# A new order of work in the first block of a transformer-layer kernel

## The reference

```
mod = silu(c) @ ada_w + ada_b                # 6 x 1024: shift1, scale1, gate1, shift2, scale2, gate2
h   = rms_norm(x, norm1_g) * (1 + scale1) + shift1
p   = h @ w_in                               # 1024 x 5384
q, k, v, f_logit, p_rwkv, gate_logit = split(p)   # 512, 512, 512, 8, 1792, 2048
log_f = log_sigmoid(f_logit + b);  cum = cumsum(log_f over tokens)
o_fox  = causal attention(q, k, v) with cum_q - cum_k added to the logits
o_rwkv = rwkv7(token_shift(p_rwkv, mu))      # token_shift(p) = p + (previous token's p - p) * mu
x = x + gate1 * ((sigmoid(gates) weighted sum of both branches) @ w_o)
x = x + gate2 * mixture_of_experts(rms_norm(x) * (1 + scale2) + shift2)
return rms_norm(x, final_g)
```

## Time and profile before

| | us |
|---|---|
| runs | 1931.38 median of 3 (1930.55 to 1931.69) |
| profiled execution, its time | 1932.95 |
| its span | 1931.2 |
| PE busy | 1744.0 (90%) |
| DVE busy | 1247.3 (65%) |
| ACT busy | 910.9 (47%) |
| POOL busy | 335.8 (17%) |
| mean granted TensorE clock | 0.949 of full |
| `front`, last evacuation starts | 567.71 |

### The profile page before, as it was taken

How to read it: one execution, slowest core, us unless ns; L and a number is a source line. 1 busy time by engine, 2 the same in 40 slices (tenths; PEclk the granted TensorE clock), 3 DMA queues, 4 the chain that set the end, 5 groups by cost and what they waited for, 6 DMA issues and landing times. The chain is left out here.

```text
span 1931.2 us, 36827 instructions
## 1 busy us (share of the span) xinstructions
PE 1744.0 (90%) x14750; PEld 1446.1 (75%) x14750; DVE 1247.3 (65%) x1663; ACT 910.9 (47%) x1347; POOL 335.8 (17%) x412
## 2 busy tenths in 40 slices
PE   5889999799989989999959989638999999999976
PEld 5568888687877868988948868426888888888862
DVE  5633255540116766777753465468999999999976
ACT  2521111122116754444431132136888888888861
POOL 1000011110012000121110001111333332333312
PEclk9889999999998989999979999859999999999997
DMA  9435566541428411010045223366899999999966
GB/s 339 152 138 204 172 221 218 207 169 44 110 73 217 96 38 38 28 53 28 15 173 199 76 91 117 125 256 241 349 381 387 386 389 381 378 390 380 377 263 255
DMA packets 116386, 393.56 MB, mean 204 GB/s; under 512 B 17889, under 2 KB 33280, under 8 KB 94752
## 3 DMA queue, kind: packets, MB, share of 16 engines
q1 hardware_dynamic: 84768, 324.05, 45.3%
q0 software_dynamic: 16736, 41.34, 5.9%
q10 hardware_dynamic: 14752, 26.29, 3.6%
HBM read 341.22 MB, written 67.18 MB: 211 GB/s over the span
## 5 line engine op out<-in xcount | busy, mean ns | idle before, releaser
L2625 DVE TENSOR_TENSOR ex_w_r<-w,ex_w_r 128x1024 fp32r<-128x1024 f32 x384 | 451.7, 1219 | 23.9 <-ACT ex_w_r L2556 10.6
L2556 ACT ACTIVATE ex_w_r<-w 128x1024 fp32r<-128x1024 f32 x384 | 404.0, 1062 | 110.0 <-PE psum L2485 87.1
L2483 PE MATMUL psum<-ex_w_r,ex_x_t 128*128 128x512 f32 x512 | 204.5, 399 | 4.0 <-DVE ex_x_t L2625 2.4
L2485 PE MATMUL psum<-ex_w_r,ex_x_t 128*128 128x512 f32 x512 | 201.3, 393 | 0.0
L2484 PE MATMUL psum<-ex_w_r,ex_x_t 128*128 128x512 f32 x512 | 200.9, 392 | 0.0
L557 ACT ACTIVATE stage<-psum 128x512 f32<-128x512 f32 (+1 forms) x72 | 41.4, 575 | 310.9 <-PE psum L153 192.1
L151 PE MATMUL psum<-w_even,h_hi 128*128 128x512 f32 (+1 forms) x320 | 118.7, 371 | 6.7 <-ACT stage L557 6.7
L152 PE MATMUL psum<-w_even,h_hi 128*128 128x512 f32 (+1 forms) x320 | 118.3, 370 | 0.0
L153 PE MATMUL psum<-w_even,h_lo 128*128 128x512 f32 (+1 forms) x320 | 118.2, 369 | 0.0
L2483 PEld LDWEIGHTS psum<-ex_w_r,ex_x_t 128*128 128x128 f32 x512 | 97.1, 190 | 23.9 <-DVE ex_x_t L2625 2.8
L2485 PEld LDWEIGHTS psum<-ex_w_r,ex_x_t 128*128 128x128 f32 x512 | 97.1, 190 | 21.1
(11 more groups left out here) (413 smaller groups left out, 4058.1 us busy)
## 6 DMA issues: line engine op xcount, KB each, us to landing
w<-in_exp_w SPq DMA_DIRECT2D x128, 1024.0 KB, 13.4
w<-in_exp_w SPq DMA_DIRECT2D x32, 2048.0 KB, 8.7
w_ring<-in_ada_w SPq DMA_DIRECT2D x12, 2048.0 KB, 10.9
w_ring<-in_w_in SPq DMA_DIRECT2D x10, 2048.0 KB, 10.3
qk<-stage_r ACTq DMA_DIRECT2D x16, 512.0 KB, 2.8
gates<-stage ACTq DMA_DIRECT2D x32, 256.0 KB, 2.3
bl_gates<-gates SPq DMA_DIRECT2D x8, 1024.0 KB, 4.8
w<-pair_rows SPq DMA_DIRECT2D x16, 512.0 KB, 10.4
```

The costliest lines, as they stand in the source:

```text
L2483: nc.tensor.matmul(out, lhs[0], hi, start=first, stop=False)
L2485: return nc.tensor.matmul(out, lhs[1], hi, start=False, stop=last)
L2556: return nc.scalar.activation(out, src, ACT.Copy)
L2625: return nc.vector.tensor_tensor(out, whole, high.bitcast(F32), ALU.subtract)
```

## The change

- The forget weights w_f are issued ahead of modulation chunks 2 and 3 and of token tiles 2 to 7.
- ACT and DVE do the eight first features and low parts without a break (w_f's split among them), then the split of the first query weights, and only then squares, means and scalings of tokens 4 to 7.
- PE's `forget(0)` comes before the first queries as it did, but each of its eight steps waits only for its own low part; all eight late flips move into the second and third query tile.
- The split of the key weights (chunk 1) and the two forget chains move behind evacuations: split at fill 1, chains behind fills 3 and 6.
- Modulation sums: chunk 4 after fill 7; 5 and 6 in the key chunk; 7, 8 and 9 in the value chunk; 10 and 11 after the first and second rwkv chunk; none after the third and fourth. The ring's order follows.
- The last two gate chunks load only when the narrow chunk's matmuls are done.
- In `attend`, values of the second head pair load before its keys.

```diff
+MOD_BEHIND = {1: (4,), 2: (5, 6), 3: (7, 8, 9), 4: (10,), 5: (11,)}
+MOD_AT = {(0, 7): 4, (1, 4): 5, (1, 7): 6, (2, 3): 7, (2, 5): 8, (2, 7): 9, (3, 7): 10, (4, 7): 11}
...
-            self.order += [c] + mod[4 + i:5 + i] if i < 8 else [c]
+            self.order += [c] + [mod[j] for j in MOD_BEHIND.get(i, ())]
...
+        FORGET_AT = (3, 6)
...
+            sp.dma_start(w_f[:], ins["w_in"][0].rearrange("(k p) n -> p k n", p=P)[:, :, COL_F:COL_R]).then_inc(sig("wf_in"), 16)
             weights.load(sp, range(2, CHUNKS))
             load_x(range(2, TT))
-            sp.dma_start(w_f[:], ins["w_in"][0].rearrange("(k p) n -> p k n", p=P)[:, :, COL_F:COL_R]).then_inc(sig("wf_in"), 16)
-            weights.load(sp, range(CHUNKS, len(weights.order)))
+            weights.load(sp, range(CHUNKS, len(weights.order) - 2))
+            sp.wait_ge(sig("proj_full"), V_TILES + 16 + RWKV_TILES)
+            weights.load(sp, range(len(weights.order) - 2, len(weights.order)))
...
-            low(0)
-            low(1)
-            mean_square(4)
-            low(2)
-            normalize(4)
-            mean_square(5)
-            low(3)
-            normalize(5)
-            dve.wait_ge(sig("wf_hi"), 1)
-            tt(wf_r[:, 1], w_f[:], wf_r[:, 0].bitcast(F32), ALU.subtract).then_inc(sig("wf_lo"), 1)
-            low(4)
-            mean_square(6)
-            low(5)
-            normalize(6)
-            mean_square(7)
-            low(6)
-            normalize(7)
-            low(7)
+            for n in range(KT):
+                if n == 2:
+                    dve.wait_ge(sig("wf_hi"), 1)
+                    tt(wf_r[:, 1], w_f[:], wf_r[:, 0].bitcast(F32), ALU.subtract).then_inc(sig("wf_lo"), 1)
+                low(n)
             for piece in range(KT // 2):
                 split_first(piece)
+            for t in range(HALF, TT):
+                mean_square(t)
+                if t > HALF:
+                    normalize(t - 1)
+            normalize(TT - 1)
             for n in range(KT, 2 * KT):
                 low(n)
-            weights.accumulate(nc, dve, link, 4, c_silu, mod_dst(4))
-            split(1)
-
-            dve.wait_ge(sig("fb_in"), 16)
-            for half in range(2):
+
+            def forget(half):
+                if half == 0:
+                    dve.wait_ge(sig("fb_in"), 16)
...
+                if half:
+                    dve.wait_ge(sig("ncum_hi"), 1)
+                    tt(ncum[:].bitcast(F32R), ncum[:], f_work[0:H], ALU.subtract).then_inc(sig("ncum_lo"), 1)
+
...
-                    if i == 1 and j >= 1 and j + 1 < len(proj):
+                    if i == 1 and j + 1 < len(proj):
                         split(j + 1)
                     m = fill - 1 - (16 + V_TILES)
                     if 0 <= m < RWKV_TILES:
                         shift(m)
-                if j < 7:
-                    weights.accumulate(nc, dve, link, 5 + j, c_silu, mod_dst(5 + j))
+                    if fill in FORGET_AT:
+                        forget(FORGET_AT.index(fill))
+                    if (j, i) in MOD_AT:
+                        weights.accumulate(nc, dve, link, MOD_AT[j, i], c_silu, mod_dst(MOD_AT[j, i]))
...
-            square(4)
-            features(1)
-            features(2)
-            square(5)
-            features(3)
             act.wait_ge(sig("wf_in"), 16)
             nc.scalar.activation(wf_r[:, 0], w_f[:], ACT.Copy).then_inc(sig("wf_hi"), 1)
-            features(4)
-            square(6)
-            features(5)
-            square(7)
-            features(6)
-            features(7)
+            for n in range(1, KT):
+                features(n)
             weights.arrived(act, weights.turn["q", 0])
             for piece in range(KT // 2):
                 ks = slice(2 * piece, 2 * piece + 2)
                 nc.scalar.activation(w_hi[0][:, ks, :], ring[:, weights.turn["q", 0] % 2, ks, :], ACT.Copy).then_inc(sig("w0_hi"), 1)
+            for t in range(HALF, TT):
+                square(t)
             for n in range(KT, 2 * KT):
                 features(n)
-            high(1)
-            act.wait_ge(sig("fb_in"), 16)
-            for half in range(2):
+
+            def forget(half):
+                if half == 0:
+                    act.wait_ge(sig("fb_in"), 16)
...
-                    if i == 1 and j >= 1 and j + 1 < len(proj):
+                    if i == 1 and j + 1 < len(proj):
                         high(j + 1)
+                    if fill in FORGET_AT:
+                        forget(FORGET_AT.index(fill))
...
-                tok = slice(half * NC5, (half + 1) * NC5)
-                pe.wait_ge(sig("h_lo"), KT * (half + 1))
+                tok, out = slice(half * NC5, (half + 1) * NC5), bank[half][0:H, :]
                 pe.wait_ge(sig("wf_lo"), 1)
-                matmul3(nc, bank[half][0:H, :], [((wf_r[:, 0, k, :], wf_r[:, 1, k, :]), (h_hi[:, k, tok], h_lo[:, k, tok]))
-                                                 for k in range(KT)]).then_inc(sig("f_full"), 1)
+                for k in range(KT):
+                    pe.wait_ge(sig("h_lo"), KT * half + k + 1)
+                    nc.tensor.matmul(out, wf_r[:, 0, k, :], h_hi[:, k, tok], start=(k == 0), stop=False)
+                    nc.tensor.matmul(out, wf_r[:, 0, k, :], h_lo[:, k, tok], start=False, stop=False)
+                    last = nc.tensor.matmul(out, wf_r[:, 1, k, :], h_hi[:, k, tok], start=False, stop=(k == KT - 1))
+                last.then_inc(sig("f_full"), 1)
...
-                    if i < 2 and k % 2 == 1 and KT + 2 + 4 * i + k // 2 < 2 * KT:
-                        flip(KT + 2 + 4 * i + k // 2)
+                    if i in (1, 2) and k % 2 == 1:
+                        flip(KT + 4 * (i - 1) + k // 2)
...
-            for n in range(KT + 2):
+            for n in range(KT):
...
             load_values(0)
+            load_values(1)
             load_keys(1, 0)
             load_keys(1, 1)
-            load_values(1)
```

More of the change, by code:

```diff
@@ L422, in _ @@
                 dve.wait_ge(sig("ncum"), half + 1)
-            dve.wait_ge(sig("ncum_hi"), 1)
-            tt(ncum[:].bitcast(F32R), ncum[:], f_work[0:H], ALU.subtract).then_inc(sig("ncum_lo"), 1)
+                if half:
+                    dve.wait_ge(sig("ncum_hi"), 1)
+                    tt(ncum[:].bitcast(F32R), ncum[:], f_work[0:H], ALU.subtract).then_inc(sig("ncum_lo"), 1)
             for j in range(len(proj)):
@@ L518, in _ @@
                 nc.scalar.activation(f_abs, f_abs, ACT.Ln, bias=1.0).then_inc(sig("f_ln"), 1)
[L519 to L524, removed]
+                if half:
+                    act.wait_ge(sig("ncum"), 2)
+                    nc.scalar.activation(f_work[0:H].bitcast(F32R), ncum[:], ACT.Copy).then_inc(sig("ncum_hi"), 1)
+                    act.wait_ge(sig("ncum_hi"), 1)
+                    act.dma_start(dram["ncum"][:, 0, :], f_work[0:H].rearrange("h a s -> h (a s)")).then_inc(sig("ncum_out"), 16)
+                    act.wait_ge(sig("ncum_lo"), 1)
+                    act.dma_start(dram["ncum"][:, 1, :], ncum[:].rearrange("h a s -> h (a s)")).then_inc(sig("ncum_lo_out"), 16)
             staged, out3 = 0, [0, 0, 0]
```

## The result

| | median, us | runs | ratio to before, 95% |
|---|---|---|---|
| before | 1930.97 | 4, 1930.44 to 1931.69 | |
| changed | 1900.40 | 4, 1899.21 to 1903.25 | 0.9844 [0.9827, 0.9861] |
| changed, in a second session | 1899.00 | 5, 1896.66 to 1902.90 (before there: 1931.43) | 0.9823 [0.9800, 0.9847] |

What follows compares the result with a forecast made beforehand. PE's waits in the first block, and slow clock after them, were taken as the loss. 21.2 + 11.5 = 32.7 us off the profiled 1932.95 gives 1900.2; that execution stood 1.6 above the median, so 1898.7, range 1893.5 to 1906.5.

Steps and rivals of the forecast that it cites:

- What can be had: PE's waits in the first block with clock lost behind two: at most 11.0 + 2.7, 8.5 and 12.2 + 2.8 us.
- First part: First block up to the fifth query tile: it starts at 84.9 instead of 104.03; 21.2 us gained with clock.
- the throughput row: DMA rate while the forget weights passed: 387 down to 285 GB/s, some 0.18 MB missing, so 0.5 us cost.
- the 1.4 us estimated from the Trainium skill: Forget weights' load: 1,024 pieces each costing like 512 B, 0.52 MB; the sum would be 0.9 us worse.
- DVE's 13.2 us: DVE's time on the first eight low halves, 41.49 to 54.70; 8.6 us without normalizations, mean squares and waiting for ACT.
- a sign: Changed profile, near 58 us: PE's wait for the last normalization should be 1.5 to 4 us in place of 8.5.
- Rival of half clock: PE in short pieces from 44 to 58 us keeps the low clock: 3.5 us lost, with ramp 5, 1904; chance 0.14.
- Forget chains: Chains behind fills 3 and 6: cost 0, ends 0 and 5 us, with 6.9 us of margin at the third tile.
- Modulation sums and ring: Value chunk: three sums there cost 0; the next projection chunk lands by 199 and is needed at 204.6.
- The slower rival: Value chunk's ring: landings beyond 29.5 us cost 2 us per us, the 32.7 are gone at 46; chance 0.03.
- Narrow chunk: First gate tile at 375.0 in place of 383.69, 8.7 us, plus 2.8 us of slow clock: 11.5 us gained.
- The term for the clock: Narrow chunk: clock loss after PE's gaps of 1.4 and 3.1 us, taken as 0.65 us, ends 0 and 2.8.

Runs made afterwards that it cites:

- The late sums: Changed kernel with modulation sums one for each chunk again from the value chunk on, the last two after the third and fourth recurrence chunk: 1909.55 us, 10.5 slower.

## Why the prediction was right

*What can be had.* Three waits and the clock behind two of them: all of it was there. The gain lies in the front: 571.92 to 539.06, 32.9 us; from there to the end the two profiles need 1359.3 and 1358.9 us. Nothing was given back. From the first flip on it is 34.0 us, and 33.2 with the second profile; the changed kernel's first profile lost 1.1 of this before its flips.

*First part, 21.2 forecast, 21.7 measured.* The fifth query tile starts at 84.99; 84.9 was worked out. That it fits to 0.1 us is in part luck. The forget weights were priced at 0.5 us, and flips did start 1.14 us later in this profile, yet across twelve profiles the place shows nothing, so the term is 0 within some 0.5 us, and neither the throughput row nor the 1.4 us estimated from the Trainium skill ("DMA: Bandwidth & Descriptors", Specifications) shows in the flips' start. From the flips on, the tokens were ready 0.5 us sooner than forecast (60.6 less 40.54, against 60.5 less 39.9). One of the forecast's terms did not come out of its own numbers: DVE's 13.2 us less 3.1, 0.6 and 1.4 are 8.1, not 8.6; it took 8.4.

DVE was said to pace the first query tile; its split ended at 55.6 (55.3 forecast), but PE was behind: 32 flips to 46.8, 24 forget matmuls of 0.23 us to 52.3, query tile to 57.9. So the wait for the tokens was 1.25 us, not 2.4, and under the 1.5 us that the forecast had named as a sign. The forecast let the forget matmuls end with the last low half at 51.3 and forgot that PE starts them only after its flips. This error left the time as it was, because PE waits for the tokens in either case. The clock, for which 0.6 us were taken, stayed full through that wait: this is the 0.5 us by which the part did better.

*Rival of half clock:* no; 1.00 from 40.54 on. The argument against it held for a stronger reason: PE had no pieces of work there, it was busy throughout.

*Forget chains, 0.* No wait between 60.69 and 333. The third tile's low half was done at 88.8 (89 forecast). The chains and the key weights' split together were worth moving: 13.5 us of front.

*Modulation sums and ring, 0 in the value chunk.* No wait there; DVE ended the split and the three sums at 170.6, 176.5, 187.2 and 193.8, where 169.6, 175.6, 186.3 and 193.5 stood. The slower rival (landing over 46 us) is far off: 14.2 at most.

*Narrow chunk, 11.5 forecast, 11.2 measured.* First gate tile at 353.59 instead of 383.69: 30.1 us, of which 21.7 are the first part's, so 8.4 here (8.7 forecast), and its clock full, about 2.8 more: 11.2. The gaps were 1.21 and 2.81 where 1.4 and 3.1 stood. The term for the clock was too small: the 24 matmuls behind the wait of 2.81 us took 4.47 us, where the same 24 take 2.97 at the full clock, so 1.5 us were lost and 0.65 priced. The late sums gave 9.8 us of the gain back, on their own they gave 9.9.

*Sum.* 32.7 forecast, 33.1 between the two profiled executions, 30.6 and 32.4 between medians. That the sum came so close is partly luck: the clock was priced 0.6 too high behind the wait for the tokens and 0.85 too low in the narrow chunk, and shorter waits made up the rest. The difference between profiles and medians is the spread of either kernel, and part of it is in the attend block, which the change hardly touches (values ahead of keys; 138.1 us before, 138.2 and 135.1 after).

## What to carry to other kernels

Find the stretch in which PE is full from end to end, and list what stands in the other engines' queues ahead of what releases it; work that is wanted much later (a forget chain, a sum over spare weights) goes behind the first evacuations and into a chunk where its engine follows nobody. Two queues that meet in one wait must be reordered together: late squares with the flips' old place made PE wait 14.68 us for the tokens, where it waited 8.50 before and 1.25 with both moved. In a sum of such steps, let each engine start a job at the later of its input and of its own queue's end.

## What was not expected of the hardware

In the changed kernel's first profile the granted clock stayed full over waits of PE of 1.21 and 1.25 us and fell after one of 2.81 us. Windows of PE around that wait (the columns as above):

```profile
346.00:349.00 3.00, 0.32 (x3) 1.00 0.16 44
349.00:352.00 3.00, 2.88 (x15) 0.62 0.39 131
352.00:355.00 3.00, 3.00 (x18) 0.82 0.31 97
```

But the length of the wait alone does not tell. The run with PE's late flips as before had the same wait of 2.81 us in the same place, and there the 24 matmuls between it and the first gate tile ran at the full clock:

```profile
363.01:365.98 2.97, 2.97 (x24) 1.00 0.39 132
```

Of ten profiles whose last narrow wait was 2.5 to 2.8 us, eight lost 1.35 to 1.5 us of clock behind it and two (2.81 and 2.51 us) nothing. With the squares back between the features the clock fell after a wait of 1.61 us that followed three of 0.55 to 0.67. A single profile therefore prices such a wait only to some 1.5 us.

A wait of DVE for a store of 64 KB of attention output behind thirteen loads of the same queue took 2.1 to 6.2 us in seven profiles with the same instructions in the block, and the block took 132.4 to 138.6 us; it was shortest where the wait was 2.1 or 2.8, longest where it was 5.6 or 6.2.
